# Branch products of a two-layer hybrid mixer in three fp32r parts, with two moves in the order of the work

## The reference

```python
def branches(oa, ob, oc, od, cols):
    return [merge_heads(oa),
            merge_heads(rms_norm(ob, hg_norm_g)) * jax.nn.silu(cols[7]),
            merge_heads(rms_norm(oc, ml_norm_g)) * jax.nn.sigmoid(cols[11]),
            merge_heads(rms_norm(od, rt_norm_g)) * jax.nn.silu(cols[16])]

def merge(outs, gate_pre):
    gates = jax.nn.sigmoid(gate_pre).reshape(gate_pre.shape[:-1] + (N_BRANCH, D_MODEL))
    acc = gates[..., 0, :] * (outs[0] @ w_branch[0])
    for n in range(1, N_BRANCH):
        acc = acc + gates[..., n, :] * (outs[n] @ w_branch[n])
    return acc @ w_out
```

## Time and profile before

| | us |
|---|---|
| median of 3 runs (lowest to highest) | 1659.28 (1655.78 to 1662.82) |
| the profiled execution, its own time | 1654.53 |
| its span (first to last instruction) | 1652.6 |
| TensorE busy | 1578.5 |
| VectorE busy | 782.8 |
| ScalarE busy | 637.5 |
| GpSimd busy | 201.6 |
| branch products, L509, 256 records (with overlap) | 93.0 |
| mean granted clock of TensorE | 0.984 |

### The profile page before, as it was taken

How to read it: one execution, slowest core, us unless ns; L and a number is a source line. 1 busy time by engine, 2 the same in 40 slices (tenths; PEclk the granted TensorE clock), 3 DMA queues, 4 the chain that set the end, 5 groups by cost and what they waited for, 6 DMA issues and landing times.

```text
span 1652.6 us, 24818 instructions
## 1 busy us (share of the span) xinstructions
PE 1578.5 (96%) x10540; PEld 1276.6 (77%) x10540; DVE 782.8 (47%) x1225; ACT 637.5 (39%) x959; POOL 201.6 (12%) x172
## 2 busy tenths in 40 slices
PE   5999999999999999899999999999999899989998
PEld 3888776765567777677777777688888668989998
DVE  4386236643633235532323223558367574565553
ACT  5623233253443234332113322452344554455452
POOL 0000002223001120121002200000004201112130
PEclk8999999999999999999999999899999999999999
DMA  8221323222031243254443535232242323445552
GB/s 354 104 103 53 134 90 115 80 72 95 33 115 58 90 160 122 92 200 172 151 180 138 193 131 198 80 128 80 84 144 71 133 92 128 160 161 197 179 181 100
DMA packets 36446, 212.83 MB, mean 129 GB/s; under 512 B 3888, under 2 KB 7344, under 8 KB 12656
## 3 DMA queue, kind: packets, MB, share of 16 engines
q1 hardware_dynamic: 36336, 211.24, 35.6%
HBM read 209.13 MB, written 2.10 MB: 128 GB/s over the span
## 4 chain that ended last, share of the span: by engine, by line
PE 88%; DVE 5%; ACT 3%; DMA 2%; issue 1%; SPq 0%; DVEq 0%; ACTq 0%
PE ps L1075 10%; PE ps L1076 10%; PE ps L1077 10%; PE ps L531 10%; PE ps L533 9%; PE ps L532 9%; PE ps L509 5%; PE ps L586 3%; PE ps L712 2%; PE ps L905 2%; PE ps L542 1%; PE ps L543 1%; PE ps L544 1%; PE ps L1020 1%; PE ps L642 1%
## 5 line engine op out<-in xcount | busy, mean ns | idle before, releaser
L531 PE MATMUL ps<-parts,whi 128*128 128x512 f32 (+1 forms) x928 | 332.1, 358 | 8.9 <-issue 4.7
L533 PE MATMUL ps<-parts 128*128 128x512 f32 (+1 forms) x960 | 330.2, 344 | 0.0
L1077 PE MATMUL ps<-parts 128*128 128x512 f32 (+1 forms) x960 | 323.0, 337 | 0.0
L532 PE MATMUL ps<-parts,whi 128*128 128x512 f32 (+1 forms) x928 | 319.0, 344 | 0.0
L1075 PE MATMUL ps<-parts 128*128 128x512 f32 (+1 forms) x928 | 315.3, 340 | 0.0
L1076 PE MATMUL ps<-parts 128*128 128x512 f32 (+1 forms) x928 | 312.5, 337 | 0.0
L1823 DVE TENSOR_TENSOR parts<-ring,parts 128x1024 fp32r<-128x1024 f32 x124 | 147.6, 1232 | 251.6 <-ACT parts L1378 251.6
L1378 ACT ACTIVATE parts<-ring 128x1024 fp32r<-128x1024 f32 x124 | 124.4, 1050 | 266.5 <-PE ps L1077 254.6
L1797 DVE TENSOR_TENSOR parts<-ring,whi 128x1024 fp32r<-128x1024 f32 (+1 forms) x136 | 162.3, 1235 | 112.5 <-ACT whi L1337 112.4
L531 PEld LDWEIGHTS ps<-parts,whi 128*128 128x128 f32 x928 | 175.9, 190 | 46.0 <-issue 24.3
L533 PEld LDWEIGHTS ps<-parts 128*128 128x128 f32 x960 | 181.6, 189 | 23.0
(11 more groups left out here) (269 smaller groups left out, 2000.5 us busy)
## 6 DMA issues: line engine op xcount, KB each, us to landing
ring<-in_w_ff SPq DMA_DIRECT2D x64, 1024.0 KB, 4.8
ring<-in_w_in SPq DMA_DIRECT2D x60, 1024.0 KB, 4.9
ring<-in_w_mod SPq DMA_DIRECT2D x40, 1024.0 KB, 4.8
arena<-in_w_mod SPq DMA_DIRECT2D x8, 1024.0 KB, 20.4
ring<-in_w_branch SPq DMA_DIRECT2D x32, 256.0 KB, 5.3
ring<-in_w_out SPq DMA_DIRECT2D x8, 1024.0 KB, 5.1
arena<-in_tables_rt SPq DMA_DIRECT2D x2, 1280.0 KB, 7.6
X<-in_x SPq DMA_DIRECT2D x2, 1024.0 KB, 6.6
```

Source lines behind the costliest of these rows:

```text
L531: pe.matmul(ps[0:m, 0:n], w_hi[:, k, c], x_hi[:, k, 0:n], start=(k == 0), stop=False)
L532: pe.matmul(ps[0:m, 0:n], w_hi[:, k, c], x_lo[:, k, 0:n], start=False, stop=False)
L533: last = pe.matmul(ps[0:m, 0:n], w_lo[:, k, c], x_hi[:, k, 0:n], start=False, stop=(k == KD - 1))
L1077: last = pe.matmul(ps[:, 0:nt], w_lo[:, k, c], x_hi[:, k, 0:nt], start=False, stop=(k == kt - 1))
```

## The change

Five things are done.

1. The branch product is made of six fp32r matmuls in place of two fp32 ones. `branch_high` on ACT copies the branch weights of a pair of tiles, 128x512, to the only buffer `whb`; it waits for the last branch product that read it. `branch_low` on DVE writes the rest. The gated outputs are first written whole (`branch_gated_whole`), to buffers that exist, then `gated_high` (ACT) and `gated_low` (DVE) make `OUT_HI` and `OUT_LO`. TensorE waits for the low weights at each even tile, and for `gated_low` at tile 0.
2. ACT handles the keys' latent (`mla_keys`) as soon as mLSTM's outputs are scaled, and copies the rotary part behind the queries' latent.
3. TensorE does ML tile 0 ahead of `retention_turn`. DVE's order of the two isn't changed.
4. The norms' table load stands ahead of the squares, in all norms but the first; `split_low(l, 1)` moves from residual 6 to behind residual 7.
5. At HGRN2's merge ACT evacuates `rg` 0, then makes the two high halves, then evacuates `rg` 1; DVE does `part_low` between the whole outputs and the low ones.

```diff
@@ -684,12 +693,20 @@
                 last_round = 1 if l == 0 else 0
                 for m in ms:
                     j, i = divmod(m, 2)
-                    slot = weights(pe, ("gate", l, n, j))
-                    wb = slot[:, 2048:2560].rearrange("p (k c) -> p k c", k=2)
+                    wb_hi, wb_lo = [w.rearrange("p (k c) -> p k c", k=2)
+                                    for w in (whb, branch_weights(low_of(l, ("gate", n, j))))]
                     parted(("gt", l, n, m), l, ("gate", n, j), i, M_HI, M_LO, nt)
                     if m == 0:
                         pe.wait_ge(*s_og.at(("og", n, l, last_round if n == ML else 1)))
-                    dense(("br", l, n, m), wb, i * P, OUT[:, n % 2], 2, nt)
+                    if i == 0:
+                        pe.wait_ge(*s_bl.at(("bl", l, n, j)))
+                    ps = bank(("br", l, n, m))
+                    c = slice(i * P, i * P + P)
+                    for k in range(2):
+                        pe.matmul(ps[:, 0:nt], wb_hi[:, k, c], OUT_HI[:, k, 0:nt], start=(k == 0), stop=False)
+                        pe.matmul(ps[:, 0:nt], wb_hi[:, k, c], OUT_LO[:, k, 0:nt], start=False, stop=False)
+                        last = pe.matmul(ps[:, 0:nt], wb_lo[:, k, c], OUT_HI[:, k, 0:nt], start=False, stop=(k == 1))
+                    last.then_inc(*product.up(("br", l, n, m)))
                     if i:
                         new_last[("gate", l, n, j)] = ("br", l, n, m)
                     else:
...
@@ -1146,8 +1163,8 @@
                     proj(l, "ql", j)
                 for g in rounds:
                     branch_turn(ML, l, g)
+                merge(l, ML, [0])
                 retention_turn(l)
-                merge(l, ML, [0])
                 if l == 0:
                     modulation_columns(PACKS[1])
...
 
             def norm(l, w):
                 n = T if (w == 0 or l == 0) else LAT
+                if w or l:
+                    act.preload_act_table_set("natural_log_exp_and_others")
...
                 if l == 0 and w == 0:
                     first_rows(0)
-                act.preload_act_table_set("natural_log_exp_and_others")
+                if l == 0 and w == 0:
+                    act.preload_act_table_set("natural_log_exp_and_others")
...
+            def branch_high(l, n, j):
+
+                i = MERGES.index((l, n, 2 * j))
+                raw = weights(act, ("gate", l, n, j))
+                if i:
+                    act.wait_ge(*product.at(("br", *MERGES[i - 1])))
+                act.activation(whb, branch_weights(raw), ACT.Copy).then_inc(*s_bh.up(("bh", l, n, j)))
+
+            def gated_high(l, n, j, raw, a):
+
+                i = MERGES.index((l, n, 0))
...
+                act.activation(o, r, ACT.Copy).then_inc(*s_oh.up(("oh", n, l, j)))
+
             def merge(l, n, ms=range(KD)):
                 nt = T if l == 0 else LAT
                 for m in ms:
                     if m % 2 == 0:
+                        if (n, m) != (ML, 0):
+                            branch_high(l, n, m // 2)
                         part_high(l, next_part(("gate", n, m // 2)))
                     ps = read(act, ("gt", l, n, m))
...
-            def mla_latents(l):
-                nt = T if l == 0 else LAT
-                last_round = 1 if l == 0 else 0
+            def mla_keys(l):
 
                 act.wait_ge(*s_og.at(("og", HG, l, 1)))
-                act.wait_ge(*s_og.at(("og", ML, l, last_round)))
                 ps = read(act, ("kv", l, 0))
                 act.activation(AKV, ps[:, :], ACT.Copy).then_inc(*s_aa.up(("kvc", l)))
                 freed(("kv", l, 0), "mla_scalar", ("kvsq", l))
                 act.activation(SQ[:, 0, :], ps[:, :], ACT.Square).then_inc(*s_aa.up(("kvsq", l)))
-                ps = read(act, ("kv", l, 1))
-                freed(("kv", l, 1), "mla_scalar", ("rope", l, 3))
-                for h in range(HEADS):
-                    act.activation(AK[64:96, h, :], ps[0:32, :], ACT.Copy).then_inc(*s_aa.up(("rope", l, h)))
+
+            def mla_latents(l):
+                nt = T if l == 0 else LAT
+                last_round = 1 if l == 0 else 0
+
                 for j in range(2):
                     ps = read(act, ("ql", l, j))
                     act.activation(AQL[:, j, 0:nt], ps[:, 0:nt], ACT.Copy).then_inc(*s_aa.up(("qlc", l, j)))
@@ -1569,6 +1609,11 @@
                         act.wait_ge(*product.at(("ot", ML, l, 0)))
                     freed(("ql", l, j), "mla_scalar", ("qlsq", l, j))
                     act.activation(QL_SQ[j][:, 0:nt], ps[:, 0:nt], ACT.Square).then_inc(*s_aa.up(("qlsq", l, j)))
+                act.wait_ge(*s_og.at(("og", ML, l, last_round)))
+                ps = read(act, ("kv", l, 1))
+                freed(("kv", l, 1), "mla_scalar", ("rope", l, 3))
+                for h in range(HEADS):
+                    act.activation(AK[64:96, h, :], ps[0:32, :], ACT.Copy).then_inc(*s_aa.up(("rope", l, h)))
...
-                for j in range(2):
-                    evac(l, "rg", j)
+                evac(l, "rg", 0)
+                for j in range(2):
+                    gated_high(l, HG, j, HGT, slice(0, nt))
+                evac(l, "rg", 1)
                 swap_halves(l)
                 merge(l, HG, [0, 1])
...
                 part_high(l, ("in", "ql"))
                 branch_tokens(l)
+                mla_keys(l)
                 part_high(l, ("gate", ML, 0))
+                for g in range(2 if l == 0 else 1):
+                    gated_high(l, ML, g, LO, slice(g * LAT, (g + 1) * LAT))
+                branch_high(l, ML, 0)
                 mla_latents(l)
...
+            def gated_low(l, n, raw):
+
+                nt = T if l == 0 else LAT
+                for j in range(2):
+                    dve.wait_ge(*s_oh.at(("oh", n, l, j)))
+                    dve.scalar_tensor_tensor(out=OUT_LO[:, j, 0:nt], in0=raw[:, j, 0:nt], scalar=1.0, in1=OUT_HI[:, j, 0:nt],
+                                             op0=ALU.mult, op1=ALU.subtract)\
+                        .then_inc(*s_og.up(("og", n, l, j)))
+
+            def branch_low(l, n, j):
+
+                a = (place[("gate", l, n, j)] % SLOTS) * SLOT
+                dve.wait_ge(*s_bh.at(("bh", l, n, j)))
+                dve.tensor_tensor(branch_weights(low_of(l, ("gate", n, j))), branch_weights(ring[:, a:a + SLOT]), whb,
+                                  ALU.subtract).then_inc(*s_bl.up(("bl", l, n, j)))
...
+                for j in range(2):
+                    dve.wait_ge(*s_ov.at(("on", n, l, j)))
+                    dve.wait_ge(*s_pa.at((name, l, j if n == HG else 1)))
+                    dve.tensor_tensor(gate[:, j, 0:nt], RS[:, j, 0:nt], gate[:, j, 0:nt], ALU.mult)\
+                        .then_inc(*s_raw.up(("raw", n, l, j)))
                 if n == HG:
                     part_low(l, ("gate", n, 0))
-                for j in range(2):
-                    dve.wait_ge(*s_ov.at(("on", n, l, j)))
-                    dve.wait_ge(*s_pa.at((name, l, 1)))
-                    dve.tensor_tensor(OUT[:, n % 2, j, 0:nt], RS[:, j, 0:nt], gate[:, j, 0:nt], ALU.mult)\
-                        .then_inc(*s_og.up(("og", n, l, j)))
+                gated_low(l, n, gate)
...
+                for g in rounds:
+                    a = slice(g * LAT, (g + 1) * LAT)
+                    dve.wait_ge(*s_oh.at(("oh", ML, l, g)))
+                    dve.scalar_tensor_tensor(out=OUT_LO[:, :, a], in0=LO[:, :, a], scalar=1.0, in1=OUT_HI[:, :, a],
+                                             op0=ALU.mult, op1=ALU.subtract)\
+                        .then_inc(*s_og.up(("og", ML, l, g)))
+                branch_low(l, ML, 0)
 
             def merge(l, n, ms=range(KD)):
                 nt = T if l == 0 else LAT
                 for m in ms:
                     if m % 2 == 0:
+                        if (n, m) != (ML, 0):
+                            branch_low(l, n, m // 2)
                         part_low(l, next_part(("gate", n, m // 2)))
                     dve.wait_ge(*s_sg.at(("sg", l, n, m)))
...
-                    if m in (4, 6):
-                        split_low(l, m // 2 - 2)
+                    if m == 4:
+                        split_low(l, 0)
+                    if m == KD - 1:
+                        split_low(l, 1)
```

36 lines of the change are left out of this document (27 added, 9 removed).

## The result

| | before | after |
|---|---|---|
| median, us | 1657.53 (4 runs) | 1689.72 (4 runs) |
| lowest to highest | 1653.56 to 1662.82 | 1680.70 to 1692.08 |
| the profiled execution, its own time | 1654.53 | 1690.90 |
| its span | 1652.6 | 1689.0 |
| mean granted clock of the profiled execution | 0.984 | 0.968 |

The ratio is 1.0184, 95% interval 1.0156 to 1.0212: the change costs 30 us by the ratio, 32 by the medians. The forecast was 1671, range 1656 to 1682. The direction was right, the size was not, and the time lies outside the range.

A forecast was written before the change was run, and what follows sets the result against it. TensorE, 96% busy, was taken to bound the kernel. Gains of -20.4 and new waits of +27.2 gave +6.8, the clock +5, together +11.8 us on the median 1659.28: 1671 us, range 1656 to 1682.

The forecast's parts named there:

- The branch product: All merge tiles: six fp32r matmuls are shorter than two fp32 ones; -12.8 in layer 0, -5.4 in layer 1, sum -16.7 us.
- The waits on the low weights: TensorE waits for new helper steps: mLSTM heads +14.0, ML tile 4 +7.6, retention's merge +3.5, start of HGRN2's merge +2.1 us.
- ML tile 4: Low weights stand behind DVE's scaling of MLA's heads: +3.6 us in layer 0, +4.0 in layer 1.
- The start of HGRN2's merge: Two low-half steps ahead of the copy that gives back TensorE's bank: +1.2 us layer 0, +0.8 layer 1, sum +2.1.
- Retention's turn: ML tile 0 and keys' latent ahead of the turn: the 2.65 us wait moves to the second gate product; -0.1 us.
- The norms: Second norms, early table load and late split: -2.8 us in layer 1, -0.8 in layer 0, sum -3.6.
- The sum without the clock: All gains, -20.4 us, and all new waits, +27.2, together: +6.8 us in TensorE's waits.
- The clock: About six new waits over 2.3 us, four dropping the clock: +6.5, less 1.5 at the last norm: +5 us.
- C: Rival: slower still, all six gaps drop the clock, longer ones twice as long; +20, 1679 us; chance 0.09.
- A: Rival: the same waits, but the clock stays up; +6.8, 1666 us; chance 0.28.
- B: Rival: faster, the waits are half and retention's turn gives its whole 3.6; -10.3, 1649 us; chance 0.12.
- D: Rival: the fp32r product isn't cheaper, so the first part is 0; +28, 1687 us; chance 0.03.

The follow-up runs named there:

- e1: Kernel before, each branch product made of six fp32r matmuls from operands already there, no added step or wait: 1649.6 us, ratio 0.9953.
- e6: Kernel before with only ML tile 0 and the keys' latent moved as in the change: 1657.7 us, ratio 1.0010.
- e7: Kernel before, its branch products of HG tiles 2, 4 and 6 waiting for a low half VectorE makes for the next block: 1692.0 us, ratio 1.0219.
- e3: Changed kernel with the low branch weights made ahead of the products of the mLSTM heads: 1667.3 us, ratio 1.0069 to before.
- e5: Changed kernel as in e3, low branch weights also early at ML tiles 4 and 6 and retention's tile 0: 1656.3 us, ratio 1.0003 to before.
- e8: As e1, but eight fp32r matmuls a tile in place of six: 1664.1 us, ratio 1.0051.
- e9: e5 with a low x low product added to the HG tiles in the mLSTM heads: 1658.5 us, ratio 1.0012 to before.
- e10: As e1, but the HG tiles in the mLSTM heads keep two fp32 matmuls; 52 of 64 products short: 1649.8 us, ratio 0.9952.
- e14: Kernel before, gate products 2, 4 and 6 of the MLA branch waiting for GpSimd's sum of the tile before: 1679.8 us, ratio 1.0140.
- e13: e5 with HGRN2's merge as before the change (fp32 products, no high or low parts): 1645.2 us, ratio 0.9942 to before.
- e11: Kernel before, only the twelve HG tiles in the mLSTM heads given six fp32r matmuls, no waits: 1662.5 us, ratio 1.0025.

## Why the prediction failed, step by step

- **The branch product**, -16.7: e1 measures -17.5 at full clock, and the periods of a tile are 6.80 and 3.61 where 6.8 and 3.6 were forecast. Right.
- **The waits on the low weights.** Heads: 3.9, 3.7, 2.5 and 2.1 forecast; 3.70, 3.43, 2.27 and 2.27 measured. The two of 0.9 in layer 0 don't show: there the clock had fallen and TensorE came late. ML tile 4: 3.6 and 5.3 against 3.39 and 5.14, and the 1.30 at L941 went, as forecast, but 1.42 came at tile 6. The start of HGRN2's merge: +1.2 and +0.8 against +1.16 and +0.6. Retention: 3.5 against 0.71 + 2.17. Right, each from one row of DVE and one of PE. MLA's tiles: no waits, as forecast.
- **Retention's turn**, -0.1: from mLSTM's turn to the second gate product 369.12 - 351.41 = 17.7 us before (the turn's start is from the trace of before), 384.00 - 366.61 = 17.4 after. Right, and e6 confirms it. The wait moved as the order said: 1.27 + 3.27 in place of 2.65.
- **The norms**, -3.6: right in the waits, not confirmed by time.
- **The sum without the clock**, +6.8: +3.6 by the runs, +3.8 by the two traces. Right within what they can tell.
- **The clock**, +5: this step failed; it measured +27. The forecast took about six waits of over 2.3 us, let four drop the clock once, at 1.7 us each, and took 1.5 back at the last norm. Two things were wrong in it. First, the price of a drop. It was taken from short stretches as at 355.00 and 1215.30. Nine at 1.7 would make 15 us, but before misses (1 - 0.984) x 1652.6 = 26 us, so others of the nine had to be longer; one of them is below. Second, what lowers the clock. The forecast let only waits do it. In the trace of after the windows at 278 and 306 us, with no wait near them, hold 11 x 0.47 + 14 x 0.48 = 12 us of missing clock by themselves, and e1 loses 9.4 us with no new wait at all. The waits are the larger part even so: e7 loses 20.8 us of clock for 15.5 us of waits in the heads, and taking the waits out of the changed kernel gives back about 18 (e3, e5). Why the clock stays down for 11 to 15 us in the heads is argued only: the heads' narrow matrices stand there. A stretch of before that the price of 1.7 us leaves out:

```profile
1055.00:1065.00 10.00, 8.60 (x19) 6.29 (x20) 6.29 (x17) 3.90 (x9) 0.00 (x0) 0.50 0.36 126
```

- **The rivals.** C, clock drops that are heavier, was the nearest; it had 0.09 and was sized at +20 in all, 1679. It too has only waits lower the clock. A, B and D fell. The Trainium skill, "TensorE: Matmul & The Clock Gate", section "HAM oscillation — how this bites in real kernels", describes groups of matmuls throttled again and again by the waits between them; the runs agree as far as the waits go, with about 18 us of clock for the changed kernel's. The falls with no wait near are beyond it. I had cited it against rival A and not let it change the price.

**What stays open:** what decides, in a stretch without any wait, whether a head's narrow matrices run at 1.2 or 2.4 GHz. e8 kept the clock with longer products, e9 didn't; e10 and e14 lost it in a head that they hadn't touched; e13 kept it. The short product seems to make such a fall more frequent (e1, e11), but four to ten runs of each, and one trace, aren't enough to give it a chance.

## What to carry to other kernels

On an engine that is 96% busy, price a new wait at its length plus the clock that it drops, and take the second part from what follows the wait: here 0.4 to 0.8 us per microsecond among wide matrices (e14) and 1.3 in the heads with their narrow ones (e7). Check such a price against the mean clock of the whole kernel before using it. Shortening products can give back through the clock part of what it saves, or more (e1, e11); here the best kernel is the one that left the heads' products and their order as they were (e13). Before adding a step on a helper engine, look in its order at what stands in front of the step and ends late; making the low weights one block of work earlier removed 13.6 us at full clock and about 18 of clock (e3, e5).

## What the runs showed of the hardware that was not expected

TensorE's clock can stand near 1.2 GHz for 11 to 15 us with the engine busy all the time by its records (278 to 289 and 306 to 320 us in the trace of after), and it does so in some executions of the kernel before too (269.8 to 283.4 us in the trace of e14, ahead of anything that e14 changes). Among 31 runs of the kernel before the mean clock goes from 0.982 to 0.991 and the time from 1664.79 to 1652.39 us with it, so most of the spread of this kernel goes with the clock. At 1.2 GHz a row of forty 128x65 matmuls takes 6.66 us for 4.68, not twice as long. And twelve products that each take 0.15 to 0.45 us less made the kernel 6.8 us slower by the medians, with an interval of the ratio that just leaves out no change (e11).
